# Expert stage of a streaming encoder layer: the first expert block's rows by one-hot products, router and experts merged into one stage, a ring of nine weight buffers

## What is computed

```python
x1 = x + (gate_a * branch_a + gate_b * branch_b) @ w_out          # 544 x 1024
n = rmsnorm(x1, g_ffn)
grp = argmax(n @ w_grp + b_grp)            # one of 4 groups of 8 experts
top_val, top_idx = top_k((n @ w_exp + b_exp)[group grp], 2)
weights = softmax(group logits)[grp] * softmax(top_val)
y = sum over the 2 chosen experts e of weights * ((silu(n @ w_e1[e]) * (n @ w_e3[e])) @ w_e2[e])
out = x1 + y
```

## Time and profile before

| | us |
|---|---|
| time, median of 3 runs | 1229.91 (1229.5 to 1231.15) |
| time of the profiled execution | 1227.32 |
| its span | 1225.5 |
| TensorE busy | 1084.5 (88%) |
| VectorE busy | 428.3 (35%) |
| ScalarE busy | 354.5 (29%) |
| GpSimd busy | 391.2 (32%) |
| mean granted TensorE clock | 0.956 of 2.4 GHz |

### The profile page before, as it was taken

The page is one execution under the profiler, slowest core; times in us unless marked ns, Lnnn a source line. Parts: engine busy times, 40 slices in busy tenths (PEclk is TensorE's granted clock), DMA queues, the critical chain, the costliest instruction groups (busy, mean ns, idle before and its releaser), DMA issues. The chain is left out here.

```text
span 1225.5 us, 20512 instructions
## 1 busy us (share of the span) xinstructions
PE 1084.5 (88%) x8243; PEld 832.5 (68%) x8243; DVE 428.3 (35%) x988; ACT 354.5 (29%) x748; POOL 391.2 (32%) x428
## 2 busy tenths in 40 slices
PE   5999899899999989999999896888888888887783
PEld 4998898798999877888898673454445444444441
DVE  6698733891111363342323442211211111111116
ACT  6547633352222644453332431000000000000000
POOL 4454458841211443322554101221212112211100
PEclk9999989898988989999999887999999999999996
DMA  7332236255322531114421898999999999999997
GB/s 130 90 83 70 69 83 167 48 158 130 91 74 61 205 103 38 50 53 139 141 79 44 304 425 354 425 428 424 430 425 429 427 429 427 429 427 430 427 427 264
DMA packets 149678, 289.10 MB, mean 236 GB/s; under 512 B 43668, under 2 KB 119028, under 8 KB 132832
## 3 DMA queue, kind: packets, MB, share of 16 engines
q1 hardware_dynamic: 94224, 249.40, 52.4%
q10 hardware_dynamic: 49632, 27.46, 8.3%
q0 software_dynamic: 5744, 11.15, 2.4%
HBM read 269.30 MB, written 26.54 MB: 241 GB/s over the span
## 5 line engine op out<-in xcount | busy, mean ns | idle before, releaser
L492 PE MATMUL bank<-xhi,cv_w_hi 128*128 128x272 f32 x848 | 260.1, 307 | 9.5 <-PEq L135 3.2
L478 POOL TENSOR_TENSOR cv_w_lo<-cv_w_raw,cv_w_hi 128x1024 fp32r<-128x1024 f32 (+1 forms) x69 | 167.9, 2433 | 310.6 <-ACT cv_w_hi L471 291.8
L2559 PE MATMUL bank<-e_w,b_xT 128*64 128x256 f32 x2048 | 231.0, 383 | 24.4 <-DVE b_xT L2588 14.9
L492 PE MATMUL bank<-xhi,cv_w_lo 128*128 128x272 f32 x848 | 251.2, 296 | 0.0
L492 PE MATMUL bank<-xlo,cv_w_hi 128*128 128x272 f32 x848 | 250.4, 295 | 0.0
L2559 PEld LDWEIGHTS bank<-e_w,b_xT 128*64 128x64 f32 x2048 | 147.3, 138 | 98.0 <-DVE b_xT L2588 19.1
L492 PEld LDWEIGHTS bank<-xhi,cv_w_hi 128*128 128x128 f32 x848 | 165.8, 195 | 18.2 <-issue 10.2
L492 PEld LDWEIGHTS bank<-xlo,cv_w_hi 128*128 128x128 f32 x848 | 166.3, 196 | 0.9
L492 PEld LDWEIGHTS bank<-xhi,cv_w_lo 128*128 128x128 f32 x848 | 165.8, 196 | 0.0
L2571 PE MATMUL bank<-e_w,b_hiddenT 128*64 128x512 f32 x512 | 116.9, 598 | 18.9 <-DVE b_hiddenT L2596 18.9
L2524 POOL COPY b_target<-slot_target 128x1 int32 (+1 forms) x31 | 5.5, 178 | 309.0 <-ACT b_y L2581 288.9
(11 more groups left out here) (447 smaller groups left out, 1641.9 us busy)
## 6 DMA issues: line engine op xcount, KB each, us to landing
e_w<-in_w_e SPq DMA_DIRECT2D x96, 2048.0 KB, 32.4
cv_w_raw<-in_w_in ACTq DMA_DIRECT2D x34, 512.0 KB, 4.2
cv_w_raw<-in_w_in SPq DMA_DIRECT2D x18, 512.0 KB, 3.9
cv_w_raw<-in_w_br_b ACTq DMA_DIRECT2D x8, 512.0 KB, 4.1
o_raw<-in_w_out SPq DMA_DIRECT2D x16, 256.0 KB, 3.7
y_rows<-choice_rows SPq DMA_DIRECT2D x8, 512.0 KB, 11.7
g_values_gates<-g_z_stage ACTq DMA_DIRECT2D x12, 272.0 KB, 4.6
f_gates<-g_values_gates SPq DMA_DIRECT2D x2, 1088.0 KB, 8.7
```

The costliest lines, as they stand in the source:

```text
L478: self.k.nc.gpsimd.tensor_tensor(self.wlo[:, s, 0:nk, :], self.raw[:, s, 0:nk, :], self.whi[:, c % OPS, 0:nk, :].bitcast(F32), ALU.subtract)\
L492: last = self.k.nc.tensor.matmul(self.bank(c, h)[:, 0:HALF], w, x[:, d, cols], start=(d == 0 and n == 0), stop=(d == nk - 1 and n == 2))
L2559: last = nc.tensor.matmul(k.bank[bank][sl[a], 0:FH], xT[:, d, :], w[slot][:, d, FH * a:FH * a + FH], start=(d == 0), stop=(d == KD - 1))
```

## The change

- The two stages become one (`choices_and_experts`): each engine runs its part of the first and then, without a barrier, its part of the second. The router's tensors and the other temporaries of the first part lie in the buffer of one weight matrix, `e_w3_3`. SyncE loads that matrix when VectorE has given `picked`, at the end of its choices.
- Block 0's rows come from the residual rows in SBUF. For each tile VectorE makes a one-hot matrix of 64 slots, scaled by the rows' inverse RMS (`first_oh`), and TensorE multiplies the residual rows by it (`first_rows`): eight products a tile, with every eighth column of the rows as weights, all forty summing into one PSUM bank, which comes out transposed as `b_xT` needs it. The indirect gather, the placing product, the add and the filler products go.
- The residual sums stay in SBUF. Their stores and loads go, and VectorE adds the choice rows onto `k.x`.
- The weights pass through nine ring buffers, three of each kind, and two more that are used once, by block 3's `w_e1` and `w_e3`. The rows' ring has three places instead of two. Seven blocks are written out ahead of the loop, and the loop has three blocks a turn.
- The sample's normed rows have a buffer of their own (`xn_s`), which overlaps `b_xT`. Block 0's `b_xT` waits until they are stored.
- The descriptor scratch of GpSimd's DMAs is halved. SiLU and product share one buffer, and other temporaries move.

The diff, cut to its core:

```diff
-RING = 4
-PAIRS = 2
+RING = 3
+EARLY = 7
...
-        k.keep_p, k.keep_s = scratch("sums_prompt", 128, 4, D), scratch("sums_sample", NS, D)
...
-        with ExitStack() as k.experts, ExitStack() as k.rings, ExitStack() as k.routing:
+        with ExitStack() as k.experts, ExitStack() as k.rings:
             expert_tensors(k)
-            k.run(project_and_choose)
-            k.routing.close()
-            k.run(expert_blocks)
+            k.run(choices_and_experts)
...
+    k.w3.append(k.sb("e_w3_3", [128, KD, FE], F32, k.rings, high=True))
...
+    k.first_oh = k.over("c_first_oh", [128, 5, SLOTS], F32, "b_rows")
+    k.sb("b_work", [128, D], F32, ctx)
+    k.xT = k.over("b_xT", [128, KD, SLOTS], F32, "b_work")
+    k.hm = k.over("b_hidden", [128, FE // 2], F32, "b_work", 4 * KD * SLOTS)
+    k.hT = k.over("b_hiddenT", [128, 2, 128], F32, "b_work", 4 * KD * SLOTS + 2 * FE)
+    k.xn_s = k.over("c_xn_sample", [128, D], F32, "b_work")
+    k.early = lambda name, *dims, dt=F32: k.within("c_" + name, [128] + list(dims), dt, "e_w3_3", size)
+    k.wr, k.br, k.gcol = k.early("w_router", KD, NL), k.early("b_router", NL), k.early("g_ffn_cols", KD)
...
-            sp.wait_ge(added1, 2)
-            sp.dma_start(k.keep_p[:, 0:2, :], k.x[:, 1:3, :]).then_inc(k.x_kept, 16)
...
-                    g.indirect_dma_start(out=k.xg[:, 0, :], out_offset=None, in_=k.halves[0:2 * NP, :],
-                                         in_offset=bass.IndirectOffsetOnAxis(ap=k.first_idx[:], axis=0),
-                                         bounds_check=2 * NP - 1, oob_is_err=False).then_inc(k.gathered[0], 16)
...
-            def keep_busy(n):
-
-                for _ in range(n):
-                    nc.tensor.matmul(P[1][:, 0:256], k.ones[:], k.wr[:].rearrange("p k n -> p (k n)")[:, 0:256], start=True, stop=True)
...
+    def on_sync(sp):
+        for j in (2 * KD - 2, 2 * KD - 1):
+            o.load(sp, j)
+        sp.wait_ge(padded, 2)
+        load_router(k, sp)
+        for e in range(2):
+            load_up(k, sp, e, e)
+            load_down(k, sp, e, e)
+        sp.wait_ge(projected, 2)
+        load_weights(k, sp, "w_e1", k.w1, k.w1_loaded, 2, 2)
+        sp.wait_ge(projected, 4)
+        load_weights(k, sp, "w_e3", k.w3, k.w3_loaded, 2, 2)
+        sp.wait_ge(projected, 5)
+        load_down(k, sp, 2, 2)
+        load_weights(k, sp, "w_e1", k.w1, k.w1_loaded, 3, 3)
+        sp.wait_ge(k.normed, 5)
+        sp.wait_ge(k.picked, 1)
+        load_weights(k, sp, "w_e3", k.w3, k.w3_loaded, 3, 3)
...
+                g.dma_start(k.table[ROW0[t]:ROW0[t] + n, :], xn_s[0:n, :]).then_inc(k.last_tabled, 16)
+        g.wait_ge(tabled, 64)
...
+        for s in range(1, RING):
+            nc.scalar.activation(k.xg[:, s, :], k.striu[:, 0:1].broadcast_to([128, D // 2]), ACT.Copy).then_inc(k.cleared, 1)
...
+        def first_rows(i):
+
+            t, n = tiles[i][1], tiles[i][3]
+            pe.wait_ge(columns, i + 1)
+            for d in range(KD):
+                last = nc.tensor.matmul(TA[:, SLOTS * d:SLOTS * d + SLOTS], k.x[0:n, t, :].rearrange("n (p k) -> n k p", k=KD)[:, d, :],
+                                        k.first_oh[0:n, t, :], start=(i == 0 and d == 0), stop=(i == 4 and d == KD - 1))
+            if i == 4:
+                last.then_inc(k.turned, 1)
...
+        place(3, tiles[3][3])
+        first_rows(0)
+        first_rows(1)
+        count(4, tiles[4][3])
+        pe.wait_ge(chosen, 6)
+        nc.tensor.matmul(L[1][:, 0:NE], k.ones[:], run[:, 1, :], start=True, stop=True).then_inc(counted, 1)
+        for i in range(2, 5):
+            first_rows(i)
+        place(4, tiles[4][3])
...
+            v.wait_ge(ranked, i + 1)
+            V.tensor_scalar(scaled[0:n, :], k.oh[0:n, 0, t, 0:1], rr[0:n, t:t + 1], None, ALU.mult)
+            c(V.tensor_scalar(other[0:n, :], r1[1][0:n, 0:SLOTS], k.oh[0:n, 1, t, 0:1], rr[0:n, t:t + 1], ALU.mult, ALU.mult))
+            V.scalar_tensor_tensor(out=k.first_oh[0:n, t, :], in0=r1[0][0:n, 0:SLOTS], scalar=scaled[0:n, :], in1=other[0:n, :],
+                                   op0=ALU.mult, op1=ALU.add).then_inc(columns, 1)
...
+        v.wait_ge(k.turned, 1)
+        v.wait_ge(k.last_tabled, 16)
+        for a in range(2):
+            f = slice(4 * a, 4 * a + 4)
+            V.tensor_tensor(k.xT[:, f], TA[:, 4 * SLOTS * a:4 * SLOTS * a + 4 * SLOTS].rearrange("p (k s) -> p k s", k=4),
+                            k.gain[:, f].unsqueeze(2).broadcast_to([128, 4, SLOTS]), ALU.mult).then_inc(k.copied, 1)
+        v.wait_ge(listed, 5)
+        c(V.tensor_tensor(sums, sums, S[:, 2 * NE:4 * NE], ALU.add))
+        V.scalar_tensor_tensor(out=k.idx[:, 0:NE], in0=sums[:, 0:NE], scalar=k.half[:, 0:1], in1=sums[:, NE:2 * NE],
+                               op0=ALU.add, op1=ALU.add)
+        V.tensor_copy(k.total[:], L[1][:, 0:NE]).then_inc(k.picked, 1)
+        v.wait_ge(k.picked, 1)
...
-        def place_first(pe):
-
-            for h in range(2):
-                last = nc.tensor.matmul(R[sl[h], :], k.first_oh[:], k.xn[0:NS, 512 * h:512 * h + 512], start=True, stop=True)
-            last.then_inc(placed, 1)
-            pe.wait_ge(joined, 1)
...
-        yrows = k.over("y_rows", [128, 5, 2, D], F32, "e_w1_0")
-        assert k.at["e_w2_0"] == k.at["e_w1_0"] + 8 * KD * FE
-        xr = k.over("x_back", [128, 5, D], F32, "e_w1_1")
...
-            eng.wait_ge(up, NE - 2)
-            eng.dma_start(xr[:, 1:5, :], k.keep_p).then_inc(x_back, 16)
-            eng.dma_start(xr[0:NS, 0, :], k.keep_s).then_inc(x_back, 16)
...
+    def loads_up(sp, e, prev, u):
+        sp.wait_ge(first, prev + 1)
+        load_weights(k, sp, "w_e1", k.w1, k.w1_loaded, e, u)
+        sp.wait_ge(up, prev + 1)
+        load_weights(k, sp, "w_e3", k.w3, k.w3_loaded, e, u)
+
+    def loads_down(sp, e, prev, d2):
+        sp.wait_ge(down, prev + 1)
+        load_down(k, sp, e, d2)
...
+    def places(b):
+
+        up_at = (b, 0) if b <= RING else ((b - 1) % RING, (b - 1) // RING)
+        return up_at + (b % RING, b // RING) + ((None, None) if b == 0 else (b % RING, b // RING - (b % RING == 0)))
...
+    yrows = k.over("y_rows", [128, 5, 2, D], F32, "late", 6 * KD * FE)
...
+    def on_sync(sp):
+        for b in range(RING + 1, EARLY):
+            loads_up(sp, b, b - RING - 1, (b - 1) % RING)
+            loads_down(sp, b - 1, b - 1 - RING, (b - 1) % RING)
+        loads_down(sp, EARLY - 1, EARLY - 1 - RING, (EARLY - 1) % RING)
+        with sp.Fori(EARLY // RING, LAST // RING) as i:
+            for s in range(RING):
+                b = RING * i + s + 1
+                loads_up(sp, b, b - RING, s)
+                loads_down(sp, b, b - RING, (s + 1) % RING)
+        loads_up(sp, NE - 1, NE - 1 - RING, (NE - 2) % RING)
+        loads_down(sp, NE - 1, NE - 1 - RING, (NE - 1) % RING)
...
+def choices_and_experts(k):
+
+    choices, experts = project_and_choose(k), expert_blocks(k)
+    with k.nc.Block() as block:
+        @block.sync
+        def _(sp):
+            choices[0](sp)
+            experts[0](sp)
...
-    nc = _bacc.Bacc("TRN2", target_bir_lowering=False, num_devices=1, dynamic_dma_scratch_size=8192)
+    nc = _bacc.Bacc("TRN2", target_bir_lowering=False, num_devices=1, dynamic_dma_scratch_size=4096)
```

More of the change, by code:

```diff
@@ new lines, in expert_blocks @@
+    last_oh = k.over("m_last_oh", [128, 5, 2 * SLOTS], F32, "c_xn")
+    last_rows = k.over("m_last_rows", [128, 5, 128], F32, "e_w1_1")
+    nothing = k.over("b_nothing", [128, D // 2], F32, "c_xn", 2 * D)
+    ohw = T("last_weight", 2, 5)
+    other = k.over("m_other", [128, 2 * SLOTS], F32, "c_xn", past)
+    b1 = k.over("m_blk_oh", [128, 10, MORE], F32, "c_xn", past)
+    cmpj, ejf = k.over("m_cmpj", [128, MORE, NE], F32, "c_xn"), T("ejf", MORE)
+    names = ("index", "first", "up", "silu", "hidden", "hturned", "hcopied", "down", "out")
@@ new lines, in products @@
+    def products(pe, b, u, nu, d2, nd, half, m):
+        if half is not None:
+            turn(pe, b, half, m).then_inc(turned, 1)
+        pe.wait_ge(copied, 2 * b + 1)
+        wait(pe, hidden, b)
+        for bank, w, loaded, made in ((1, k.w1, k.w1_loaded, first), (2, k.w3, k.w3_loaded, up)):
+            pe.wait_ge(loaded[u], 16 * nu + 16)
+            for d in range(KD):
+                if bank == 1 and d == 4:
+                    pe.wait_ge(copied, 2 * b + 2)
+                for a in range(2):
+                    last = nc.tensor.matmul(k.bank[bank][sl[a], 0:FH], xT[:, d, :], w[u][:, d, FH * a:FH * a + FH],
+                                            start=(d == 0), stop=(d == KD - 1))
+            last.then_inc(made, 1)
+        pe.wait_ge(hidden, b + 1)
+        for c in range(2):
+            last = nc.tensor.transpose(k.bank[3][:, 128 * c:128 * c + 128], hm[:, c:FH:2], k.ident[:])
+        last.then_inc(hturned, 1)
+        pe.wait_ge(hcopied, b + 1)
+        pe.wait_ge(k.w2_loaded[d2], 16 * nd + 16)
+        wait(pe, out, b)
+        for f in range(NF):
+            for a in range(2):
```

(12 more changed lines are left out.)

1093 lines of the change are left out of this document (497 added, 596 removed).

## The result

The changed kernel takes 1234.07 us (median of 20 runs, 1228.21 to 1240.04) where the kernel before takes 1229.7 (20 runs on the same chips). The ratio is 1.0031, with a 95% interval from 1.0016 to 1.0045: slower by 3.8 us by that ratio [2.0 to 5.5], where I had forecast 1.0 us less. Two executions of later kernels, of 1265.81 us (before without restore) and 5829.43 us (buffers used twice), are slow ones and are left out of their ratios.

A forecast was written before the change was run, and what follows sets the result against it. The expert weight stream, a DMA queue served in order at 427 GB/s, was taken as the bound. Restart +5.3 us and restore -6.3 us gave -1.0 us: median 1229.91 becomes 1228.9 us, range 1218 to 1236.

The forecast's parts named there:

- so the twelfth issue is in time and no second hole opens: Weight queue at block 0: first product ends about 757.4, one matrix takes 4.9 us (753.5 to 758.4), so no further gap.
- the things costed at nothing: Added VectorE operations, sample's table rows, block 1's gathers, nine ring buffers and three-block loops: all hidden, 0 us.
- so the queue stays filled: Nine ring buffers instead of twelve: three blocks of lead less the matrix in use still some 35 us, costing nothing.
- The restart, +5.3: Eleventh matrix, waiting on `picked` after the one-hot products, is issued at 752.8 instead of 747.50: +5.3 us, between +4.5 and +6.5.
- 17.5: TensorE's 40 one-hot products, 80 records at the lower clock: 18.0 us less 0.5 for a later clock fall.
- rival two: One-hot products' strided weights cost 1.67 times: 0.376 us a record, 30.1 us, +12.1, 1241.0 us; decides from 0.27; chance 0.20.
- The restore, -6.3: Tail of the queue: residual-row loads no longer precede the choice rows; 6.3 us saved by landings, 5.2 by bytes.
- One: Rival: one-hot products stay at 2.4 GHz, 9.0 us; restart -4.0, with the restore -10.3, 1219.6 us; chance 0.20.
- Three: Rival: GpSimd's halved descriptor scratch makes gathers wait for scatters, 18 us a block against 14.7, about 100 us more; chance 0.03.
- four: Rival: ring lead too short, each steady block loses some 0.7 us between landing and issue, +19 us; chance 0.04.
- Hidden work: VectorE's added operations (at most 1.2 us), the sample's table rows and block 1's gathers hide behind other work, 0 us.

The follow-up runs named there:

- before without restore: The kernel before without the two loads that bring the residual rows back, their stores kept; ratio to the kernel before 0.9953.
- buffers used twice: The changed kernel with its two single-use weight buffers used once more, for block 7, and ten blocks written out; ratio to the kernel before 1.0005.
- the second execution: The changed kernel run again with no edit, beside other variants; ratio to the kernel before 1.0024.
- the run with adjacent weights: The changed kernel with one-hot products reading 128 adjacent columns of residual rows as weights instead of every eighth; ratio to the kernel before 1.0010.
- the swap: The changed kernel with one-hot columns as weights and residual rows moving, 10 products instead of 40, then copy and transposes; ratio to the kernel before 0.9955.
- the filler run: The changed kernel with four filler products of 256 columns ahead of the first one-hot product; ratio to the kernel before 1.0039.

## Why the prediction was wrong, step by step

**The step that failed** is "so the twelfth issue is in time and no second hole opens", and with it the line among the things costed at nothing that three blocks of lead are some 35 us, "so the queue stays filled". The twelfth issue was in time (757.95, while the eleventh, which landed 8.6 us after its issue, was still moving). I took that for the whole of the matter. I set the twelfth issue against 757.33 in the kernel before, which is its thirteenth, and I used the landing times of the steady state, 32 to 44 us, for a stretch in which the queue had no backlog: from 752 to 794 the matrices of the changed kernel whose landing the trace gives took 8.6 to 14.3 us. There the number of matrices ahead of TensorE decides, and block 3 is followed by one issue where every other block is followed by three. The row of the queue at 793.72 would follow from the diff alone: single-use buffers are used once, so one block gives no buffer back. Price: 2.3 us in the windows, 1.6 at the sums, shown by the kernel in which it is gone (by the ratios 3.2, with overlapping intervals).

**The restart, +5.3.** The mechanism was right and the size too small. From the projections' end the eleventh matrix is issued 25.7 us later (752.41 - 726.68), before 18.8: +7.0, and +6.4 in the second execution. The one-hot products carry it: 19.7 us where I had 17.5, and the run with adjacent weights puts 1.9 of the 2.2 on the stride. So rival two was real, at 0.246 us a record, below the 0.27 from which I let it decide.

**What the restart is worth** I had as one for one. It isn't. Eleven matrices stand ahead of block 0, and the twelfth needs block 0's first product. 12.4 us earlier gave 1.4; 5.8 us later cost 1.9. What counts is block 0's start: the swap moved it by 6.8 us in the profile and left all behind it as it was. In the changed kernel both hang on the same products. So that the restart could stand in the sum at its full size was luck.

**The restore, -6.3.** Measured -5.1 by the profile and -5.8 by the runs. I put the missing 0.5 to 1.2 down to the latency of the first choice rows, which used to be hidden by the restore; no run shows it by itself.

**The sum again**: +6.4 to +7.0 restart, +2.3 second hole, -5.1 restore, together +3.6 to +4.2; measured +3.8 [2.0 to 5.5]. Its terms are read from single executions, and where each has 1 to 2 us of its own, the close fit is partly luck.

**The rivals.** One (the upper level, 1219.6) didn't happen: 0.50 in every window from 730 to 756, and the filler run shows that the products are no quicker where it is higher. The Trainium skill (TensorE: Matmul & The Clock Gate, "Why this matters for your kernels") says that keeping TensorE continuously busy keeps it at the full clock; by the window 742 to 752, busy for 10.00 of 10.00 us at 0.50, this trace disagrees, as the earlier trace rows did. Three (GpSimd's scratch) and four (a loss in each steady block) didn't happen: 427 GB/s from 814 to 1160. But four named the right suspect, the shorter lead, and looked for it in the wrong blocks. The kernel before with its down matrix one block late shows that a matrix of lead at block 0 is worth about 4 us of the stream on its own (3.7 by the restore's landing, 4.8 in the windows).

**Hidden work.** VectorE's added operations, the sample's table rows and block 1's gathers cost nothing that can be seen: block 0's xT waits for the products alone (10.64 us). One wait ahead of them I had not in the sum. ScalarE's scaling of the last prompt tile waits 6.22 us for a table store (4.66 before), and TensorE then waits 0.89 us for `c_xT` (0.52 before); in the swapped kernel it was 8.86 and 1.95. Why these stores land later wasn't looked into.

## What to carry to other kernels

When a ring loses depth, don't judge it by the landing times of the steady state: count, block by block from the first consumer on, how many transfers are issued and how many have moved, above all where a buffer is used once and gives nothing back. Ask of a gap in a queue which event it is measured from; here the consumer's start moved the end in full by the profile, and the gap's own end by a tenth to a third. And a transfer taken from the tail is worth its time less the latency that it was hiding.

## What the runs showed of the hardware

At a granted clock of 0.50 a record of 128 columns of weights at a stride of eight elements took 0.246 us, with adjacent columns 0.222. At a granted clock of 0.95 and 0.90 the strided ones were as slow as at 0.50.

Swapped, with 512 strided columns moving, 8 records took 3.92 us with the clock at 0.50 and 12 took 5.83 us with it at 0.92 to 1.00: 0.49 each at either level. A down product of the blocks, also 512 moving columns against 64 of weights but adjacent, is 16 records in 3.65 us at the upper level, 0.23 each. At the lower level adjacent moving columns were no quicker: the four records of L2545 in the kernel before (512 columns, 32 rows deep) took 1.97 us, 0.49 each. So by these rows the stride costs a tenth on the weights and nothing on the moving side at the lower level, and takes away the whole gain of the upper one. That the stride is the cause at the upper level wasn't tried by itself. The windows of the two groups in the swapped kernel:

```profile
736.00:738.00 2.00, 2.00 (x8) 0.28 (x4) 0.38 (x3) 0.00 (x0) 0.00 (x0) 0.50 1.05 444
740.00:742.00 2.00, 2.00 (x6) 0.16 (x2) 0.00 (x0) 0.00 (x0) 0.00 (x0) 1.00 0.92 387
```

The first transfers behind an idle queue start slowly: 123 and 279 GB/s in the windows 752 to 756, about 1.7 us less than the full rate would have moved from 752.41 on. The kernel before has the same behind its own idle stretch (197 and 393 GB/s in 748 to 752, from 747.50 on), so it is no part of the difference.
